# Later groups of two feed-forwards' first matrix: two output tiles by seven half-size products instead of eight

## The reference

```python
def hybrid_layer(x, w_in, w_out, w_ff1, w_ff2, ...):
    ...
    x = layernorm(DEEPNORM_ALPHA * x + mix, ln1_g, ln1_b)
    hid = jnp.square(jax.nn.relu(jnp.einsum('bsd,df->bsf', x, w_ff1)))   # 1024 -> 4096
    ff = jnp.einsum('bsf,fd->bsd', hid, w_ff2)                           # 4096 -> 1024
    return layernorm(DEEPNORM_ALPHA * x + ff, ln2_g, ln2_b)
```

## Time and profile before

| | before |
|---|---|
| median of 3 runs | 2080.28 us (2080.08 to 2080.41) |
| profiled execution: time, span | 2081.08 us, 2079.3 us |
| PE busy | 2052.4 us (99%), 9744 matmul records |
| DVE busy | 1097.8 us (53%), 1794 instructions |
| ACT busy | 922.7 us (44%), 1502 instructions |
| bytes moved by DMA | 211.37 MB, 102 GB/s on the mean |
| TensorE clock granted | 0.998 of full |

### The profile page before, as it was taken

One profiled execution on the slowest core, in us unless ns is written; L12 is line 12 of the kernel. 1 busy time (PEld: TensorE's weight loads), 2 busy tenths in 40 slices (PEclk: granted clock), 3 DMA queues, 4 the chain that ended last, 5 costly groups with the idle time before them and its releaser, 6 DMA issues. The chain is left out here.

```text
span 2079.3 us, 24586 instructions
## 1 busy us (share of the span) xinstructions
PE 2052.4 (99%) x9744; PEld 1692.3 (81%) x9744; DVE 1097.8 (53%) x1794; ACT 922.7 (44%) x1502; POOL 150.5 (7%) x207
## 2 busy tenths in 40 slices
PE   9999999999999999999999999999999999999997
PEld 6888788888888888788688888888888788888886
DVE  6655566565343444477586333337677585333336
ACT  5664334334232322366357243344566357233243
POOL 0000000000000000354000000000353000000000
PEclk9999999999999999999999999999999999999999
DMA  7332222333333322633332333322632332332321
GB/s 241 99 105 62 81 66 97 124 100 122 103 100 102 102 81 62 183 109 90 116 102 82 101 102 101 102 81 62 178 102 81 117 102 88 109 99 90 101 81 41
DMA packets 201518, 211.37 MB, mean 102 GB/s; under 512 B 7803, under 2 KB 181115, under 8 KB 201404
## 3 DMA queue, kind: packets, MB, share of 16 engines
q1 hardware_dynamic: 194544, 194.13, 29.9%
q0 software_dynamic: 6352, 15.24, 2.8%
q10 hardware_dynamic: 508, 0.43, 0.1%
HBM read 194.55 MB, written 8.95 MB: 98 GB/s over the span
## 5 line engine op out<-in xcount | busy, mean ns | idle before, releaser
L619 PE MATMUL ps<-Phi,wh 128*128 128x512 f32 (+1 forms) x1200 | 475.9, 397 | 5.0 <-DVE x_fvv L1236 2.2
L622 PE MATMUL ps<-Phi,wl 128*128 128x512 f32 (+1 forms) x1200 | 455.2, 379 | 0.6 <-DVE wl L1153 0.6
L620 PE MATMUL ps<-Plo,wh 128*128 128x512 f32 (+1 forms) x1200 | 454.4, 379 | 0.0
L1153 DVE TENSOR_TENSOR wl<-stage,wh 128x1024 fp32r<-128x1024 f32 x249 | 303.5, 1224 | 69.9 <-ACT wh L1923 51.5
L1923 ACT ACTIVATE wh<-stage 128x1024 fp32r<-128x1024 f32 (+2 forms) x252 | 260.4, 1041 | 172.4 <-PE ps L622 157.5
L619 PEld LDWEIGHTS ps<-Phi,wh 128*128 128x128 f32 x1200 | 226.2, 189 | 55.2 <-issue 12.6
L622 PEld LDWEIGHTS ps<-Phi,wl 128*128 128x128 f32 x1200 | 225.6, 188 | 44.4 <-DVE wl L1153 1.0
L620 PEld LDWEIGHTS ps<-Plo,wh 128*128 128x128 f32 x1200 | 226.3, 189 | 40.6 <-issue 4.1
L619 PE MATMUL ps<-Qhi,wh 128*128 128x512 f32 (+1 forms) x680 | 256.6, 377 | 0.7 <-DVE Qlo L1169 0.7
L620 PE MATMUL ps<-Qlo,wh 128*128 128x512 f32 (+1 forms) x680 | 254.4, 374 | 0.0
L622 PE MATMUL ps<-Qhi,wl 128*128 128x512 f32 (+1 forms) x680 | 254.4, 374 | 0.0
(11 more groups left out here) (301 smaller groups left out, 2934.3 us busy)
## 6 DMA issues: line engine op xcount, KB each, us to landing
stage<-in_w_ff SPq DMA_DIRECT2D x64, 1024.0 KB, 5.3
stage<-in_w_in SPq DMA_DIRECT2D x39, 1024.0 KB, 5.3
stage<-in_w_up SPq DMA_DIRECT2D x16, 1024.0 KB, 5.4
stage<-in_w_down SPq DMA_DIRECT2D x16, 1024.0 KB, 5.2
stage<-in_w_in SPq DMA_DIRECT2D x30, 512.0 KB, 5.1
stage<-in_w_out SPq DMA_DIRECT2D x12, 1024.0 KB, 5.3
stage<-in_w_bg SPq DMA_DIRECT2D x4, 1024.0 KB, 5.2
vrev<-H SPq DMA_DIRECT2D x2, 2048.0 KB, 13.9
```

What stands on the lines that cost most here:

```text
L619: e.matmul(o, hi[:, k, cs_], hi_x[:, kx, tok], start=k == 0, stop=False)
L620: e.matmul(o, hi[:, k, cs_], lo_x[:, kx, tok], start=False, stop=False)
L622: t = e.matmul(o, lo[:, k, cs_], hi_x[:, kx, tok], start=False, stop=k == nk - 1)
L1153: t = e.tensor_tensor(lo, src, hi.bitcast(F32), ALU.subtract)
```

## The change

For F = 1 and 2 and the groups g = 1, 2, 3, the eight up tiles are made in four pairs by a scheme of seven products (`PRODUCTS`, `quad`). The pair's weights are a 2 by 2 matrix of quarters (two halves of k, two tiles), x a 2 by 2 matrix of quarters (two halves of k, two halves of the tokens). Each product is one 4-block sum over a quarter, 128 features by 256 tokens: 4 blocks times 3 matmuls of 128x256. They run in the order Q1, Q6, Q5, Q7, Q2, Q3, Q4. Q2 accumulates onto the bank of Q1, Q3 onto that of Q5, Q4 onto that of Q7, after VectorE or ScalarE has read those. Sums of quarters take the place of the eighth product:

- sums of x's quarters (`xs1` to `xs4`, VectorE; high part by ScalarE, low by VectorE) are made once a feed-forward, in group 0;
- sums of the weight quarters (`ws`, VectorE: `weight_sums`) are made for each pair, and then split like any weights. A pair has four pieces, three of 128x1024 and one of 128x512, where it had two of 128x1024;
- the results are put together from PSUM: U, V, c22, c12, c21 on VectorE, Q1's copy (`q1`) and c11 on ScalarE, then relu, square and split for two hidden tiles.

A pair prepares the pieces of the next one while it runs: the sums after U, the subtractions behind V, c22 and c12.

The two relus in place wait for VectorE's c12 and c21, and the copies of weight sums for VectorE's sums. The core of the diff:

```diff
+PRODUCTS = (("Q1", 2, 0, 0), ("Q6", 1, 0, 1), ("Q5", 0, 4, 2), ("Q7", 0, 0, 3), ("Q2", 2, 4, 0), ("Q3", 1, 4, 2),
+            ("Q4", 3, 0, 3))
...
             for g in range(4):
-                self.cols(w_ff1[L], 1024 * g, 1024 * g + 1024)
+                (self.cols if g == 0 else self.fours)(w_ff1[L], 1024 * g, 1024 * g + 1024)
...
+    def quad(self, x, product, after):
+        i, base = self.used, 4 * ((self.quads + 1) % 2)
+        self.used += 4
...
+        for name, piece, k0, bank in PRODUCTS:
+            b = base + (self.banks + bank) % 4
+            for k in range(4):
+                product(i, name, piece, b, k0, k)
+                self.tick()
+            after(i, name, b)
+            if name == "Q6":
+                while self.prepared < i + 7 and self.ready():
+                    lows.append(self.prepare(True))
+            if name in ("Q5", "Q3") and lows:
+                lows.pop(0)()
+            if name == "Q7":
+                while lows:
+                    lows.pop(0)()
+            if name in ENDS:
+                self.release(i + piece)
+            if name == "Q7" and self.prepared < i + 8:
+                lows.append(self.prepare(True))
...
+                    again = {"Q2": act_x["q1", F, g, p], "Q3": vec_x["V", F, g, p], "Q4": vec_x["c22", F, g, p]}
+                    if k == 0:
+                        on.wait_ge(*([again[name]] if name in again else free[b]))
...
+            def weight_sums(second, third):
...
+                e.tensor_tensor(ws[u][:, :, :, :], one, other, ALU.add).then_inc(*w_low.up("sum", i))
+                on.wait_ge(w_low["sum", i])
+                e.tensor_tensor(ws[v][:, 0], ws[u][:, 1], a, ALU.add).then_inc(*w_low.up("sum of three", i))
+                on.wait_ge(w_low["sum of three", i])
+                e.tensor_tensor(ws[v][:, 1], ws[v][:, 0], b, ALU.add).then_inc(*w_low.up("sum", i + 1))
...
             def ff(F, first, begun, whole):
                 for g in range(4):
-                    for j in range(begun if g == 0 else 0, 8):
+                    if F and g == 0:
+                        w.beside.append(spaced([*(lambda m=m: x_sum(2 * F - 2, m) for m in (1, 3, 2, 4)),
+                                                *(lambda m=m: x_sum_low(F, m) for m in (1, 3, 2, 4))], 4))
+                        w.pace = 1.0
+                    for j in range(begun if g == 0 else 0, 0 if F and g else 8):
                         w.gemm("P", 8, nothing, ev_up(F, g, j))
+                    if F and g == 0:
+                        w.finish()
+                    for p in range(4 if F and g else 0):
+                        w.quad("P", nothing, combined(F, g, p))
```

More of the change, by code:

```diff
@@ L173, in values, with fours @@
                 self.slab(src, k, k + 4, c, c + 512, "V")
+    def fours(self, src, c0, c1):
+        v = src.rearrange("(k p) c -> p k c", p=128)
+        for c in range(c0, c1, 256):
+            n = len(self.slabs)
+            self.sums |= {len(self.pieces), len(self.pieces) + 1}
+            self.pieces += [(n, 0, cut) for cut in ((0, 8, 0, 128), (0, 8, 0, 128), (0, 8, 0, 128), (4, 8, 128, 256))]
+            self.slabs.append([(v[:, :, c:c + 256], 8, 256, 0)])
     def width(self, i):
@@ L191, with __init__ @@
 class Walk:
-    def __init__(self, weights, own, high=None, low=None):
+    def __init__(self, weights, own, high=nothing, low=nothing, sums=nothing):
         self.weights, self.own = weights, own
-        self.high, self.low = high, low
+        self.high, self.low, self.sums = high, low, sums
+        self.quads = 0
         self.ring, self.slot, self.freed = [0, 1, 2, 3], {}, [None] * 7
@@ L226, in release, with ready @@
             self.ring.append(self.slot[i])
+    def ready(self):
+        return self.prepared < len(self.weights.pieces) and len(self.ring) > (self.prepared in self.weights.sums)
     def prepare(self, apart=False):
[L229 to L236, removed]
+        if not self.ready():
+            return nothing if apart else None
+        slots = []
+        for i in range(self.prepared, self.prepared + (2 if self.prepared in self.weights.sums else 1)):
+            self.prepared += 1
+            u = self.slot[i] = self.ring.pop(0)
+            slots.append((i, u, self.freed[u]))
+        if len(slots) == 2:
+            self.sums(*slots)
+        for slot in slots:
+            self.high(*slot)
         def rest():
-            if self.low:
-                self.low(i, u, freed)
+            for slot in slots:
+                self.low(*slot)
         if apart:
@@ L248, in piece @@
         most = max(self.prepared + 1 + (i + 1) % 2, i + 1) + more
-        while self.prepared < min(i + (ahead or self.ahead) + more, len(self.weights.pieces), most) and self.ring:
+        while self.prepared < min(i + (ahead or self.ahead) + more, len(self.weights.pieces), most) and self.ready():
             self.prepare()
@@ L359, in spaced @@
         f()
-def nothing(*args):
-    return None
 class Heads:
@@ L650, in tile_tok, with product, step, produced @@
                 return step
+            def product(F, g, p):
+                def step(i, name, piece, b, k0, k):
+                    u = w.slot[i + piece]
+                    _, hi, lo = weights.tiles(i + piece, stage, wh, wl, u)
+                    o = banks[b][:, 0:256]
+                    if name in ("Q1", "Q2", "Q3"):
+                        kx, sl = k + (0 if name == "Q1" else 4), HALVES[name == "Q3"]
+                        x, y = Phi[:, kx, sl], Plo[:, kx, sl]
+                    else:
+                        m = {"Q5": 1, "Q6": 2, "Q7": 3, "Q4": 4}[name] - 1
+                        on.wait_ge(vec_x["T low", F, m + 1])
+                        x, y = x_high[m][:, k, :], x_low[m][:, k, :]
+                    again = {"Q2": act_x["q1", F, g, p], "Q3": vec_x["V", F, g, p], "Q4": vec_x["c22", F, g, p]}
+                    if k == 0:
+                        on.wait_ge(*([again[name]] if name in again else free[b]))
+                    on.wait_ge(w_high[i + piece])
+                    e.matmul(o, hi[:, k0 + k, :], x, start=k == 0 and name not in again, stop=False,
+                             skip_group_check=name in again)
+                    e.matmul(o, hi[:, k0 + k, :], y, start=False, stop=False, skip_group_check=name in again)
+                    on.wait_ge(w_low[i + piece])
+                    t = e.matmul(o, lo[:, k0 + k, :], x, start=False, stop=k == 3, skip_group_check=name in again)
+                    if k == 3:
+                        t.then_inc(*gemm.up("product", i, name))
+                return step
+            def produced(F, g, p):
+                def after(i, name, b):
+                    events = {"Q6": vec_x["U", F, g, p], "Q2": act_x["c11", F, g, p], "Q3": vec_x["c12", F, g, p],
+                              "Q4": vec_x["c21", F, g, p]}
+                    if name in events:
+                        free[b] = [events[name]]
+                return after
             def frees(*events):
@@ L1160, in low @@
                 e.memset(both[:, :, m:32].bitcast(F32), 0.0).then_inc(*w_low.up(i))
-            w = Walk(weights, DVE, low=low)
+            def weight_sums(second, third):
+                (i, u, freed), (_, v, freed_v) = second, third
+                n = weights.pieces[i][0]
+                a, b = (stage[n % 2][:, 1024 * j:1024 * j + 1024].rearrange("p (k c) -> p k c", k=4)[:, :, 0:128]
+                        for j in range(2))
+                one, other = (bass.AP(tensor=stage[n % 2][:, :].tensor, offset=o, ap=[[2048, 128], [step, 2], [256, 4], [1, 128]])
+                              for o, step in ((0, 128), (128, 1024)))
+                on.wait_ge(landed(i), *slot_over(freed), *slot_over(freed_v))
+                e.tensor_tensor(ws[u][:, :, :, :], one, other, ALU.add).then_inc(*w_low.up("sum", i))
[3 more added lines that the diff above has]
+                e.tensor_tensor(ws[v][:, 1], ws[v][:, 0], b, ALU.add).then_inc(*w_low.up("sum", i + 1))
+            w = Walk(weights, DVE, low=low, sums=weight_sums)
             h_over = [[] for _ in range(8)]
@@ L1920, in high @@
             def high(i, u, freed):
-                src, hi, _ = weights.tiles(i, stage, wh, wl, u)
-                on.wait_ge(landed(i), *slot_over(freed))
+                src, hi, lo = weights.tiles(i, stage, wh, wl, u)
+                if i in weights.sums:
+                    src = ws[u][:, :, :, :].rearrange("p j k c -> p (j k) c")
+                    on.wait_ge(w_low["sum", i], *slot_over(freed))
+                else:
+                    on.wait_ge(landed(i), *slot_over(freed))
                 e.activation(hi, src, ACT.Copy).then_inc(*w_high.up(i))
@@ L2202, in ev_down, with x_sum_high, combined, squared @@
                 return evict
+            def x_sum_high(F, m):
+                on.wait_ge(vec_x["T sum", F, m])
+                t = e.activation(x_high[m - 1][:, :, :], x_sums[m - 1][:, :, :], ACT.Copy)
```

(36 more changed lines are left out.)

69 lines of the change are left out of this document (66 added, 3 removed).

## The result

The changed kernel takes 2090.36 us (median; 2089.41 to 2091.86), the kernel before 2080.28 (2080.08 to 2080.41). The ratio is 1.0047, with a 95% interval of 1.0034 to 1.006: slower by 10 us where 2077 was forecast, and outside the range of 2068 to 2086. The profiled execution took 2089.41 us with a span of 2087.6, which is 8.3 us more than the 2079.3 of before.

A forecast was written before the change was run, and what follows sets the result against it. TensorE's full stream was taken as the bound: 19.2 us removed, some 15.8 returning as waits in pairs 2 and 3, leaving 3.4 saved from 2080.28, about 2077 us. Its own range was 2074 to 2080.5; 8 in 10, 2068 to 2086.

The forecast's parts named there:

- The pairs: Four up-tile pairs per later group: 42.95 us against 43.52, saving 0.57 a group, 3.4 us over six groups.
- TensorE's 0.12 a matmul: New 128x256 products in the pairs: 0.12 us per matmul, 53% of a full one's price, so 10.08 us a pair.
- The turn from c12 to c12: VectorE-ScalarE loop in a pair: 0.46 + 3.63 + 7.66 = 11.75 us, which TensorE cannot pass; pair 3 takes it whole.
- Costed at nothing. The token sums: Beside group 0's last four up tiles: 8 x 1.15 us VectorE, 4 x 0.95 ScalarE, free under VectorE's 3.26 us idle per tile.
- 9.2 us twice: Price of the token sums in group 0 if VectorE's idle time did not cover them.
- A (2061): Pairs: TensorE keeps its 0.12 pace through most because the turn is shorter than added up; 19.2 us saved, 2061; chance 0.13.
- the argument against A: Pairs: the order leaves VectorE nothing to do between c21 and the hidden subtractions.
- B: Pairs: no neighbours on VectorE or ScalarE overlap, each step costs full duration; turn 12.52 us, total 2085.4; chance 0.20.
- The rule of the Trainium skill that was weighed there: VectorE empties its pipe after every instruction before the next starts, so instruction count matters; pairs go from 4 to 14.
- C (a late slab): Pair 4: slab over 2 us later than the trace's 5.74, down tile waits for eighth hidden tile; e.g. 2089; chance 0.07.

The follow-up runs named there:

- experiments 1: Changed kernel with ScalarE's copies and VectorE's low parts of the token sums moved to group 0's down tiles, VectorE's sums spaced one per up tile: 2076.97 us.
- experiment 3: Changed kernel with the same work beside the same four up tiles, but ScalarE's copies of the token sums starting one tile later: 2076.74 us.
- experiment 4: Changed kernel with token-sum copies and low parts beside the down tiles, plus weight sums for the pair after next made before the two hidden subtractions: 2061.64 us.
- sums_alone: Kernel before plus only the token sums, in the changed kernel's order and unused; all tiles made by eight full products: 2093.15 us.

## Why the prediction was wrong

**The pairs: right.** TensorE's 0.12 a matmul held. The turn from c12 to c12 is 1206.34 to 1218.01, 11.67 us, forecast 11.75. By the starts of their first matmuls, pair 2 takes 10.99 us (1195.89 to 1206.88; forecast 11.04) and pair 3 11.67 (1206.88 to 1218.55; forecast 11.75), and pairs 1 and 4 take 10.1 each and lose nothing. PE's listed idle time in pairs 2 and 3, 0.65, 0.18 and 0.91, is less than the loss from start to start, and it stands at c22, V and c22 as forecast. A group gained 0.68 us where 0.57 was forecast, and six 4.1 where 3.4 was. With the sums of x out of the way (experiments 1 and 3) the kernel takes 2076.97 and 2076.74: the forecast's 2077.

**The step that failed: "Costed at nothing. The token sums".** It set 8 x 1.15 us of VectorE and 4 x 0.95 of ScalarE against the 3.26 us in which VectorE idles at each tile, and took the idle time for cover. The 3.26 us is what one of these four tiles had. At the other three VectorE idled less before its hidden subtraction in the kernel before:

```profile
1122.80 0.69 DVE L1169 TENSOR_TENSOR Qlo<-f,Qhi 128x512 fp32r<-128x512 f32 x1 [0.59 <-ACT Qhi L1940]
...
1128.24 0.69 DVE L1169 TENSOR_TENSOR Qlo<-f,Qhi 128x512 fp32r<-128x512 f32 x1 [3.21 <-ACT Qhi L1940]
...
1133.68 0.69 DVE L1169 TENSOR_TENSOR Qlo<-f,Qhi 128x512 fp32r<-128x512 f32 x1 [2.13 <-ACT Qhi L1940]
```

With the 3.26 that makes 9.2 us, no more than the 8 x 1.15 of the sums. Still, the amount is not what failed: experiment 3 puts the same work beside the same four tiles, and PE does not wait for it. What failed is the step from idle time to cover. The row also says whom that idle time waits for: ScalarE's copy of the hidden tile. An instruction queued behind that wait on VectorE, whose result ScalarE copies ahead of its next relu, adds to the turn that makes the wait. Its price without cover was put at 9.2 us twice; the turn made it 6.0 and 6.2, of which 3.3 are the lower granted clock behind the waits, which the prediction had nowhere. A sum of busy times could not have caught it, since the relation is in the two orders: the prediction drew the order of both engines for a pair and not for group 0.

**The rivals.** A (2061) names the time that experiment 4 reached, but not its reason: the turn is as long as the prediction added up; it had to be shortened by moving the weight sums into VectorE's idle time, the very gap that the argument against A names. B falls: pair 3 takes 11.67 us and not over 12.2, and neighbours overlap with the waits met. In a pair, the sum at 1211.36 follows U at 1211.03 by 0.33 with a duration of 0.41; in group 0, the subtraction at 1134.91 follows the one at 1133.77 by 1.14 with a duration of 1.23, and the sum follows by 1.14 again. An instruction that needs the one before does start behind its whole duration, as the sums at 1200.12 and 1201.37 do (1.25 apart, the first of 1.22). The rule of the Trainium skill that was weighed there (VectorE: DVE Perf Modes, "The DRAIN you can't avoid"), that the next instruction does not start until the pipe is empty, is not what the first of these rows show. The same section of the Trainium skill has an exception that the prediction left out: "A next op that is not held starts earlier". With that these rows agree. C (a late slab) gave as its sign that the first down tile waits for hidden tiles, and that sign came, but in group 0, where there are no pairs, and with sums_alone, where no slab is read in another way. In the six later groups no down tile waits. So a symptom that was named for one cause had another: the releaser of the releaser has to be read too.

**What stays open.** The median of the timed runs is 10.1 us over before, the profiled execution only 8.3: the one of before took 0.8 more than its median, and the one of the changed kernel is the fastest of its runs, 1.0 under the median. The length of the slow stretch behind the wait differs between executions: about 9 matmuls twice here, but 14 and 7 in the profile of sums_alone, whose waits were the same. That may be why the times differ from one execution to the next; no run shows it.

## What to carry to other kernels

An engine's idle time is no cover for work that stands behind the wait and on which the awaited partner depends, as the sums did here; write out both orders and follow one turn through them before a step is costed at nothing. Between two engines that work in order, let the consumer take a result one tile after the producer makes it: here two empty places in a list were worth 13.6 us. And in a loop between two engines, put the independent work in front of the instruction that waits, not behind it: that was worth another 15.3 us (2076.97 to 2061.64).

## What the runs showed of the hardware

Waits of 3.4 and 4.3 us in the middle of a dense stream cost more than themselves here. In the changed kernel PE stood from 1141.5 to 1145.3 and again had 0.70 us of full pace; then the granted clock fell to the lower of its two levels, 1.2 GHz:

```profile
1145.30:1146.00 0.70, 0.70 (x3) 0.61 (x4) 0.70 (x1) 0.00 (x0) 0.00 (x0) 1.00 1.08 385
1146.00:1149.50 3.50, 3.50 (x11) 2.68 (x10) 3.50 (x5) 1.99 (x2) 0.00 (x0) 0.52 0.23 78
1149.50:1155.00 5.50, 5.50 (x26) 4.53 (x25) 2.51 (x3) 0.01 (x1) 0.00 (x0) 0.99 0.59 191
```

Over 1146.0 to 1149.5 it is 0.52, matmuls of 512 columns start 0.43 apart instead of 0.2267, and from 1149.76 on they are back at 2.4 GHz. In F = 2 the distance is 0.43 at once, from 1770.59 to 1774.00. That cost 1.6 and 1.7 us at the two waits. The Trainium skill (TensorE: Matmul & The Clock Gate, "Wait — 56ns, not 53.3ns?") gives 426.7 ns as the distance at 512 columns and 1.2 GHz, which these rows confirm. A matmul of 256 columns with its own weights kept its 0.12 us, 53% of a full one, through every later group, and a sum over strided halves on VectorE takes 1.22 us, as long as the plain subtraction of the earlier trace rows, which was taken for it.
